# Lower halves of the weight blocks made by GpSimd in the loop of the token mixer

## The reference, cut to what matters

```python
def token_mixer(h, w_in, ...):
    proj = h @ w_in + b_in                      # 1024 -> 6 x 1024
    x_rnn, y_rnn, glu_v, glu_g, gate_a, gate_b = jnp.split(proj, IN_SPLITS, axis=-1)
    xr = causal_depthwise_conv(x_rnn, rnn_conv_w, rnn_conv_b)        # 4 taps
    xr = rg_lru(xr, rg_w_a, rg_b_a, rg_w_x, rg_b_x, rg_lambda)       # heads of 256, a scan over tokens
    y_a = (xr * jax.nn.gelu(y_rnn)) @ rnn_w_proj
    v = glu_v * jax.nn.sigmoid(glu_g)
    v = causal_depthwise_conv(v, conv_dw_w, conv_dw_b)               # 31 taps
    v = jax.nn.silu(layernorm(v, conv_ln_g, conv_ln_b))
    y_b = v @ conv_w_proj + conv_b_proj
    merged = jax.nn.sigmoid(gate_a) * y_a + jax.nn.sigmoid(gate_b) * y_b
    return merged @ w_out
```

## Time and profile before

| | |
|---|---|
| median of 3 runs | 2747.86 us (2746.51 to 2750.76) |
| the profiled execution | 2748.82 us, its span 2747.2 us |
| busy in the span | PE 2564.4, PEld 2191.1, DVE 1625.9, ACT 1027.7, POOL 13.1 us |
| mixer's loop, first `vpad` to last `cv` | 1871.6 to 2199.3 us of the span |
| granted TensorE clock over the span | 0.977 of full |

### The profile page before, as it was taken

The page is one execution under the profiler, slowest core; times in us unless marked ns, Lnnn a source line. Parts: engine busy times, 40 slices in busy tenths (PEclk is TensorE's granted clock), DMA queues, the critical chain, the costliest instruction groups (busy, mean ns, idle before and its releaser), DMA issues.

```text
span 2747.2 us, 40135 instructions
## 1 busy us (share of the span) xinstructions
PE 2564.4 (93%) x14516; PEld 2191.1 (80%) x14516; DVE 1625.9 (59%) x2388; ACT 1027.7 (37%) x1349; POOL 13.1 (0%) x28
## 2 busy tenths in 40 slices
PE   6999999999999988999899999989999889999996
PEld 2788888888888775888688999988888757788885
DVE  5567777777777754333345443457999855534445
ACT  3334443444344323333234322235455533542222
POOL 0000000000000000000000000000000000000000
PEclk9999999999999998999899999999999999999998
DMA  5212211121112222222122222222222212222232
GB/s 219 69 62 76 70 61 61 62 83 61 61 53 89 79 85 69 69 69 69 45 94 74 91 87 92 92 92 85 89 87 91 85 54 88 89 99 92 92 99 84
DMA packets 59817, 224.34 MB, mean 82 GB/s; under 512 B 6496, under 2 KB 6496, under 8 KB 59136
## 3 DMA queue, kind: packets, MB, share of 16 engines
q1 hardware_dynamic: 56544, 207.94, 22.3%
q0 software_dynamic: 3232, 15.86, 1.5%
HBM read 221.68 MB, written 2.10 MB: 81 GB/s over the span
## 4 chain that ended last, share of the span: by engine, by line
PE 79%; DVE 9%; ACT 5%; issue 5%; DMA 1%; DVEq 0%; ACTq 0%; SPq 0%; POOL 0%
PE ps L409 71%; PE ps L568 3%; ACT w_hi L812 2%; PE ps L590 1%; DVE K L1469 1%; PE ps L466 1%; DVE w_lo L1265 1%; DVE cv L1826 1%; ACT K_now L932 1%; PE ps L581 1%; ACT L910 1%; DVE f_tree L1461 1%; DMA ada_raw<-in_ada_weights_dram 1%; PE ps L609 1%; DVE n_tmp L1826 0%
## 5 line engine op out<-in xcount | busy, mean ns | idle before, releaser
L1265 DVE TENSOR_TENSOR w_lo<-w_raw,w_hi 128x1024 fp32r<-128x1024 f32 x360 | 440.2, 1223 | 618.2 <-ACT w_hi L812 616.4
L812 ACT ACTIVATE w_hi<-w_raw 128x1024 fp32r<-128x1024 f32 x360 | 381.2, 1059 | 973.3 <-PE ps L409 939.5
L409 PE MATMUL ps<-n_hi,w_hi 128*128 128x512 f32 (+1 forms) x992 | 323.8, 358 | 29.7 <-DVE w_lo L1265 15.4
L409 PE MATMUL ps<-n_lo,w_hi 128*128 128x512 f32 (+1 forms) x992 | 320.2, 355 | 0.0
L409 PE MATMUL ps<-n_hi,w_lo 128*128 128x512 f32 (+1 forms) x992 | 319.8, 354 | 0.0
L409 PE MATMUL ps<-h_hi,w_hi 128*128 128x512 f32 x640 | 273.0, 427 | 9.2 <-DVE h_lo L1292 4.6
L409 PE MATMUL ps<-h_hi,w_lo 128*128 128x512 f32 x640 | 255.0, 398 | 0.0
L409 PE MATMUL ps<-h_lo,w_hi 128*128 128x512 f32 x640 | 254.8, 398 | 0.0
L409 PEld LDWEIGHTS ps<-n_hi,w_hi 128*128 128x128 f32 x992 | 175.4, 191 | 65.9 <-issue 20.2
L409 PEld LDWEIGHTS ps<-n_lo,w_hi 128*128 128x128 f32 x992 | 176.0, 190 | 26.7 <-issue 0.2
L409 PEld LDWEIGHTS ps<-n_hi,w_lo 128*128 128x128 f32 x992 | 175.8, 190 | 26.6
(11 more groups left out here) (327 smaller groups left out, 5012.9 us busy)
## 6 DMA issues: line engine op xcount, KB each, us to landing
w_raw<-in_weights_dram SPq DMA_DIRECT2D x376, 512.0 KB, 3.3
ada_raw<-in_ada_weights_dram SPq DMA_DIRECT2D x4, 2048.0 KB, 25.2
gate_raw<-in_gate_weights_dram POOLq DMA_DIRECT2D x16, 512.0 KB, 4.8
x<-in_x_dram SPq DMA_DIRECT2D x1, 2048.0 KB, 9.3
x<-in_x_dram POOLq DMA_DIRECT2D x1, 2048.0 KB, 11.1
out_dram<-fin POOLq DMA_DIRECT2D x1, 2048.0 KB, 6.5
xc<-in_ctx_dram POOLq DMA_DIRECT2D x1, 1024.0 KB, 10.7
F_raw<-in_seq_dft_dram POOLq DMA_DIRECT2D x1, 1024.0 KB, 5.5
```

The lines of the kernel that those rows point to most:

```text
L409: last = nc.tensor.matmul(o, w, xp, start=start and n == 0, stop=stop and n == 2)
L812: run(w_hi[:, s], w_raw[:, s], ACT.Copy).then_inc(hi_ready[s], 1)
L1265: tt(w_lo[:, s], w_raw[:, s], w_hi[:, s].bitcast(F32), ALU.subtract).then_inc(lo_ready[s], 1)
```

## The change

GpSimd gets a loop over the mixer's four iterations, with a `tensor_tensor` subtract for 12 of the 14 blocks of an iteration. VectorE keeps `after(5)` and `after(8)`, the cuts of blocks 7 and 10, which follow the short products 6 and 9. (Number 14, 15 and 16 in `BY_POOL` are blocks 0, 1 and 2 of the next iteration.) GpSimd waits for `hi_ready` as VectorE did, and gives the same `lo_ready`. Nothing else moves; the cut of block 2 ahead of the loop stays with VectorE, and so do all blocks outside the mixer's loop.

```diff
+BY_POOL = (3, 4, 5, 6, 8, 9, 11, 12, 13, 14, 15, 16)
+BLOCKS_TO_MIX = HEADS * 6 + 2 * KD + 4 * GROUPS + 2 * KD + 2 * FT + len(FF_GROUPS) * KD
...
             pool.dma_start(meta[:], meta_in).then_inc(meta_in_s, 16)
+            st = Stream()
+            st.base = BLOCKS_TO_MIX
+            with pool.Fori(0, KD // 2) as i:
+                st.enter(i, 14)
+                for m_ in BY_POOL:
+                    s, use = st.slot(m_)
+                    pool.wait_ge(hi_ready[s], use + 1)
+                    nc.gpsimd.tensor_tensor(w_lo[:, s], w_raw[:, s], w_hi[:, s].bitcast(F32), ALU.subtract
+                                            ).then_inc(lo_ready[s], 1)
+            st.leave(KD // 2)
             pool.wait_ge(NOUT["lo"], KD)
             pool.dma_start(out, fin[:]).then_inc(out_s, 16)
...
-                after(1)
                 product(0)
                 some_taps(5)
-                after(2)
                 some_taps(5)
-                after(3)
...
-                after(4)
                 for a in range(2):
                     actv(1 + a)
...
                 some_taps(4)
                 after(5)
                 some_taps(6)
-                after(6)
                 some_taps(3)
-                after(7)
                 some_taps(6)
                 after(8)
                 some_taps(2)
                 product(1)
                 some_taps(2)
-                after(9)
                 some_taps(2)
-                after(10)
...
                 some_taps(4)
-                after(11)
                 for a in range(2):
                     actv(5 + a)
...
                 some_taps(2)
-                after(12)
                 some_taps(6)
...
-                after(13)
                 some_taps(7)
-                after(14)
                 some_taps(len(taps))
```

## The result

The changed kernel takes 2800.5 us (median), the kernel before 2749.3 beside it: 1.0182 times as long, 95% interval 1.0161 to 1.0202. That is +51 us where I had forecast +32, and 2.5 us above the upper end of my range. The direction and the mechanism came as forecast; the size did not.

What follows compares the result with a forecast made beforehand. In the mixer's loop TensorE was taken to wait for VectorE, whose cuts queue behind taps. Blocking by GpSimd's reads, less absorbed idle time, gave +32.5 us: 2781.3, less 1 us for the runs' median, so 2780; range 2721 to 2798.

Steps and rivals of the forecast that it cites:

- What VectorE loses: In the mixer's loop, 47 of the 48 cuts leave VectorE's stream at 1.13 us each, freeing 53 us.
- What GpSimd gets: Each cut on GpSimd takes 2.1 to 2.5 us, with 2.6 as upper bound.
- What it does to the taps: VectorE's taps may stand while GpSimd reads SBUF, each cut then costing GpSimd's whole time instead of 1.13 us; chance 0.60.
- L: VectorE's time lost to each GpSimd cut in the loop, set equal to GpSimd's time for it; 2.2 us taken.
- The sum in the blocked case: Loop growth of 47 x (L - 1.13), less VectorE idle time that fills up: +32.5 us at L = 2.2.
- Is GpSimd's cut in time?: GpSimd has 4.1 us for a cut, 2.8 at block 13, so latency costs nothing unless it takes 3 us or more.
- room to run a block or two at the lower clock: TensorE, with 74.8 us of work in an iteration of some 89, could run some blocks slower.
- GpSimd starved: Rival: overlapping taps keep GpSimd out until VectorE waits, TensorE stands still; some +60 us, 2808; chance 0.05.
- the likeliest case: VectorE can't work while GpSimd reads SBUF in the loop; 2762 to 2800 us, chance 0.60.
- What would show it.: Profile signs: GpSimd busy 100 to 120 us, caught taps of 2 to 3, iteration about 89, clock below 0.98.
- no blocking: Rival: both engines read side by side, taps keep 0.67 us, TensorE becomes the bound; -25 us, 2723; chance 0.25.
- partial sharing: Rival: the port is shared by turns, VectorE losing 1.4 to 1.8 us a cut; 2740 to 2761 us; chance 0.10.

Runs made afterwards that it cites:

- pause_for_8: The changed kernel with one wait added: VectorE stops at the old place of block 8's cut until GpSimd has made it; 2779.9 us.
- aside_read: The kernel before, all cuts on VectorE, plus 48 GpSimd subtracts on scratch data at the cuts' times, not awaited in the loop; 2810.7 us.
- run 5: The changed kernel with four taps of each iteration's first half (16, 20, 24, 28) waiting for the tap just ahead; 2783.1 us.
- aside_write: The kernel before, all cuts on VectorE, plus 48 GpSimd memsets of 128x1024 on scratch at the cuts' times; 2751.0 us.

## Why the prediction was right in kind and too small

*What VectorE loses* held: 48 instructions less, each 1.13 us of its stream; three cuts or eight, the account closes with it.

*What GpSimd gets* held: 2.1 to 2.5 us forecast, 2.40 measured for a cut that begins just as a tap ends (longer records contain the rest of that tap). By the estimate of 2.25 us from the Trainium skill (GPSIMD Engine Reference, section 3.1) I would have been 0.15 low, by the middle of my bounds 0.1.

*What it does to the taps* held: L = 2.2 forecast, 2.15 measured. That it is so close is luck. I had set L to GpSimd's whole time for a cut, and that is 2.40 us, of which VectorE loses 0.25 less. With the true 2.40 my own sum would have given 47 x 1.27 - 16.1 = +43.6 us, some 2791.

*The sum in the blocked case* held in total: 47 x (2.15 - 1.13) = 47.9 us of growth, against which 17.9 us of idle time were to fill up; the growth without starvation is 27.7 us, so 20 us were absorbed. They lie where VectorE had waited: 3.3 us of 4.1 in each `xr_lo` to `ii` (13 us), 5.4 at the loop's end with its 3.05 us for `w_hi`, some 1.3 at its start, and none from `ii` to `xr_lo`. pause_for_8 at 2779.9 us is the test of that sum, against 2780. That they agree so closely is partly chance, since the pause has small costs and a half-starved cut of its own (8.41 us at 2044.34).

*Is GpSimd's cut in time?* failed for 6 cuts of 48. Three are those of block 15, late behind ScalarE as told above, and cost nothing; the cases that I had named for it (a cut of 3 us or more, block 13) didn't come. The other three are the starved ones: I counted GpSimd's time from the moment its input is ready and set the starting of it at nothing. Of the whole cost, 24 of 51.7 us came from there. I also gave TensorE "room to run a block or two at the lower clock". Over the iteration it has that room, but not at block 8, on whose end the chain to `ii` hangs: 6.8 of the 24 us are block 8's slower matmuls.

**The step that failed is the rival "GpSimd starved", set at nothing in the likeliest case.** I had named its mechanism (taps that overlap and never let GpSimd in until VectorE waits), but as a case that excludes the others, for every cut or for none, with a chance of 0.05. It happens beside blocking, now and then. So it belonged in the likeliest case as a term: some cuts, each at the rest of VectorE's run. The place was in my own working: I had counted the 15 taps between the cuts of blocks 7 and 10 as one run, with the cuts of 8 and 9 in the midst of it, and took for granted that GpSimd would get in. My price for one cut was small as well: 6 taps, 4 us, where they stood for 8.9 to 9.6 us. Two such cuts at 8 us each would have put the time at about 2796.

*What would show it.* Busy GpSimd 100 to 120 us: 142, of which 20 are starved waiting (an estimate: the three long records above 2.5 us each). Taps of 2 to 3 us where caught: yes, 2.89. An iteration of 89 us: 31.9 + 58.7 = 90.6 undisturbed, 96.5 and 98.6 with a starved cut. Larger waits at `xr_lo`: yes, 27.4 us in four. Waits behind GpSimd's blocks gone: no, 23.1 us, 15.3 of them for starved cuts. Clock below 0.98: 0.90 over the loop, and 0.98 still in the first iteration. The rivals "no blocking" and "partial sharing" are refuted by VectorE's records: one tap of 2.83 to 2.90 us for each cut that catches one, and 0.74 to 0.75 for all others with two inputs. The 1.64 us of aside_read lie in the range that I had given to sharing, but they come the same way, as one tap of 2.38 us beside a subtract of 1.89.

What stays open is the exact condition of starvation. The traces show a bundle (VectorE unbroken, overlapping, for a while since GpSimd's last turn); one gap of 0.2 us ended it at block 8, but I have no run that varies only the length of the run, and the cuts named in run 5 had equal distances and unlike outcomes. Whether a small difference in time against the taps decides is not tested.

## What to carry to other kernels

Work handed to GpSimd is not free for VectorE if GpSimd reads SBUF while VectorE works on two SBUF inputs: price each instruction at nearly GpSimd's own duration (2.15 of 2.40 us here) against what it cost on VectorE (1.13), and hand over only what reads no SBUF or falls into VectorE's waits. Then look for VectorE's longest run without a wait: an instruction of GpSimd that another engine needs can stand there until the run ends, and one short wait in the run let it in here at block 8. Where an engine is late for a few signals, moving those few ahead of work that nobody awaits was worth more here (-7.5 us) than any share of it given away.

## What the runs showed of the hardware

- GpSimd's subtract of 128x1024 takes 2.40 us at its shortest (2.36 right behind another) with two different inputs, and costs VectorE 2.15 us. Where both inputs are the same 512 columns read twice over (aside_read) it takes 1.89 us and costs 1.64. Why that one is shorter no run shows: its inputs are narrower, and its output is another type.
- A memset of 128x1024 by GpSimd takes 0.96 us and leaves the taps with two inputs alone. But the first tap of a half, with one input, took 1.32 us beside one and not 0.55, once an iteration; VectorE's timeline of aside_write:

```profile
1954.30 1.32 DVE L1840 TENSOR_SCALAR cv<-vpad,vec 128x512 f32 x1 [0.32 <-DVE vpad L1859]
```

  The stretch from `ii` to `xr_lo` is 0.8 us longer for it (51.4). The same page and section of the Trainium skill has one-input instructions in their faster two-port modes contend with GpSimd, which would account for that; no run here tries it by itself.
- Who issues first doesn't tell the whole story of this pair. The Trainium skill (SBUF — State Buffer, section Who interferes with whom) has the second one blocked until the first is done. For the taps that holds. GpSimd mostly gets in when the running tap ends, with the next one due 0.66 us behind it, but three times it was passed over by about ten taps in a row (8.92 to 9.60 us), which start behind GpSimd's record; when each was issued the trace doesn't show.
- A blocked instruction counts as busy in the records: VectorE's busy time rose by 20.6 us while it did 48 instructions less. Busy time going up on the engine that lost work was itself the sign of it here.
